# Reordering the stage between the projection and the attention of a hybrid decoder layer

## The reference

```
h = RMSNorm(x) * (1 + scale1(c)) + shift1(c)
p = h @ w_in
NSA group   (8 query heads, 2 kv heads): compressed-block, gathered top-k selected-block and
            sliding-window (512) branches, mixed by per-head sigmoid gates
mLSTM group (4 heads): matrix memory C, normaliser n, running-max stabiliser
pool group  (4 channel groups): trailing means over 2/4/8/16 positions, per-group linear map
x = x + gate1(c) * (concat(nsa, mlstm, pool) @ w_out)
h = RMSNorm(x) * (1 + scale2(c)) + shift2(c)
x = x + gate2(c) * ((silu(a) * b) @ w_down),  [a, b] = causal depthwise conv3(h @ w_up)
```

## Time and profile before

| | us |
|---|---|
| median of 3 runs (lowest, highest) | 848.26 (846.79, 848.85) |
| the profiled execution | 852.0 |
| its span in the trace | 850.1 |
| PE busy | 784.1 (92% of the span) |
| DVE busy | 508.4 (60%) |
| ACT busy | 329.0 (39%) |
| POOL busy | 307.6 (36%) |

### The profile page before, as it was taken

The page is one execution under the profiler, slowest core; times in us unless marked ns, Lnnn a source line. Parts: engine busy times, 40 slices in busy tenths (PEclk is TensorE's granted clock), DMA queues, the critical chain, the costliest instruction groups (busy, mean ns, idle before and its releaser), DMA issues.

```text
span 850.1 us, 18842 instructions
## 1 busy us (share of the span) xinstructions
PE 784.1 (92%) x7517; PEld 723.3 (85%) x7517; DVE 508.4 (60%) x1026; ACT 329.0 (39%) x601; POOL 307.6 (36%) x163
## 2 busy tenths in 40 slices
PE   2899989998989798998988999999999999999994
PEld 2798979988967565668988999999999999999993
DVE  3655888974494798763566566665212666665324
ACT  3332322322341356653235445443113455444221
POOL 0042656553000144461432344344444344343440
PEclk9899999998797699998999999999999999999997
DMA  9964867885569744305720333333323333322212
GB/s 354 332 214 136 252 221 254 288 263 163 201 217 385 141 120 122 102 2 174 292 98 28 122 105 120 114 105 105 94 81 112 123 101 112 100 78 97 89 56 100
DMA packets 73142, 131.23 MB, mean 154 GB/s; under 512 B 12685, under 2 KB 47389, under 8 KB 72801
## 3 DMA queue, kind: packets, MB, share of 16 engines
q1 hardware_dynamic: 66928, 114.32, 41.8%
q10 hardware_dynamic: 6096, 15.73, 5.2%
q0 software_dynamic: 32, 0.00, 0.0%
HBM read 124.56 MB, written 9.12 MB: 157 GB/s over the span
## 4 chain that ended last, share of the span: by engine, by line
PE 71%; DVE 12%; issue 6%; DMA 4%; POOL 3%; ACT 2%; SPq 2%; ACTq 0%; DVEq 0%; POOLq 0%
PE ps L668 53%; PE ps L1016 2%; PE ps L1001 2%; DMA arena<-cache_keys 2%; PE ps L1038 2%; POOL arena L612 2%; PE ps L1054 2%; PE ps L919 1%; DMA arena<-weights 1%; POOL wR L631 1%; PE ps L686 1%; DMA raw<-weights 1%; DVE arena L2079 1%; DVE arena L1504 1%; SPq L475 1%
## 5 line engine op out<-in xcount | busy, mean ns | idle before, releaser
L668 PE MATMUL ps<-hR,wR 128*128 128x260 f32 x3456 | 432.9, 287 | 11.5 <-POOL wR L631 3.6
L668 PEld LDWEIGHTS ps<-hR,wR 128*128 128x128 f32 x3456 | 426.2, 192 | 15.7 <-issue 10.7
L631 POOL TENSOR_TENSOR wR<-raw,wR 128x1024 fp32r<-128x1024 f32 x92 | 223.4, 2429 | 308.5 <-ACT wR L1136 308.5
L1136 ACT ACTIVATE wR<-raw 128x1024 fp32r<-128x1024 f32 x94 | 99.4, 1058 | 213.5 <-PE ps L668 210.0
L668 PE MATMUL ps<-fR,wR 128*128 128x260 f32 x1056 | 128.1, 283 | 2.2 <-DVE fR L2050 2.0
L668 PEld LDWEIGHTS ps<-fR,wR 128*128 128x128 f32 x1056 | 127.0, 188 | 3.1 <-DVE fR L2050 2.4
L2074 DVE COPY arena<-arena 128x2 f32<-128x2 f32 x44 | 47.6, 1082 | 93.6 <-ACT arena L1427 93.6
L624 POOL TENSOR_SCALAR arena<-arena,fac 128x128 f32<-128x128 f32 (+3 forms) x32 | 40.3, 1263 | 138.7 <-DVE fac L1973 138.7
L612 POOL TENSOR_TENSOR arena<-arena,par 128x512 f32<-128x512 f32 x32 | 43.6, 1369 | 72.7 <-DMA arena<-cache_keys 65.7
L2035 DVE TENSOR_TENSOR t<-ps,mod 128x8 f32<-128x8 f32 x24 | 4.0, 167 | 108.6 <-PE ps L668 108.6
L1360 ACT ACTIVATE arena<-ps,nmx 128x128 f32<-128x128 f32 (+3 forms) x64 | 33.2, 526 | 20.0 <-DVE nmx L1964 20.0
(11 more groups left out here) (369 smaller groups left out, 829.3 us busy)
## 6 DMA issues: line engine op xcount, KB each, us to landing
raw<-weights SPq DMA_DIRECT2D x95, 512.0 KB, 3.7
arena<-cache_keys SPq DMA_DIRECT2D x128, 192.0 KB, 3.5
arena<-weights SPq DMA_DIRECT2D x27, 512.0 KB, 9.5
arena<-cache_values SPq DMA_DIRECT2D x128, 64.0 KB, 2.0
raw<-weights ACTq DMA_DIRECT2D x12, 512.0 KB, 8.0
arena<-weights ACTq DMA_DIRECT2D x9, 512.0 KB, 7.5
x<-xT SPq DMA_DIRECT2D x16, 260.0 KB, 4.2
out_y<-x SPq DMA_DIRECT2D x8, 260.0 KB, 2.2
```

Source lines behind the costliest of these rows:

```text
L631: nc.gpsimd.tensor_tensor(w_slot(i)[:, 1, :, :], raw[:, g % RAW, :, :], w_slot(i)[:, 0, :, :].bitcast(F32), ALU.subtract).then_inc(lo_read ...
L668: last = mm(ps[:, a + half, 0:TH], w_slot(i)[:, wp, k, :], src[:, hp, j, half * TH:(half + 1) * TH], start=(j == 0 and q == 0), stop=(j == ...
L1136: A(w_slot(i)[:, 0, :, :], raw[:, g % RAW, :, :], ACT.Identity).then_inc(hi_ready, 1)
```

## The change

It leaves the arithmetic and moves instructions between the projection and the attention:

- PE: the block sums (L825) come ahead of triple 0; triples 1 to 7 stand earlier among the pieces, the gate columns behind the sample rows; the sample rows take 4 matmuls of 192 columns in place of 4 of 128 and 4 of 64; the pool group's map moves ahead of triple 7 and to other PSUM banks; the three last turns stand together, and the heads' transposes come last of all.
- DVE: the samples' block maxima and their ranking move forward, the compressed weights and the weighting of the samples' rows ahead of the last two heads; `side_mix` is gone, and the multiplication into `mix` is the last piece before L1900.
- SP: the gate rows leave before the window keys; the window keys go as six samples after the 15th half of the pages and two after the 16th (before: four and four after the 16th); SP issues the weight tiles of triples 2 to 7; the values of samples 0 and 1 come behind those; the window values of samples 0 and 1 now wait for `mmix_ready` and come before three weight tiles of the output projection and the small outputs.
- ACT: issues no weights, and its pieces follow PE's new order.

```diff
-            sp.wait_ge(comp_done, 2 * NB)
-            sp.wait_ge(slc_scored, 2 * NB)
-            for b in range(0, NB, 4):
-                sp.dma_start(kwin[:, b:b + 4, :], winK[:, b:b + 4, :]).then_inc(win_landed, 16)
+            sp.wait_ge(rows_ready, 1)
+            sp.dma_start(spread, mro[0:4, :]).then_inc(side_landed, 16)
+            for half, first, last in ((2 * NB - 1, 0, 6), (2 * NB, 6, 8)):
+                sp.wait_ge(comp_done, half)
+                sp.wait_ge(slc_scored, half)
+                sp.dma_start(kwin[:, first:last, :], winK[:, first:last, :]).then_inc(win_landed, 16)
...
+            load_rows(2)
+            load_rows(3)
+            for g in range(N_A + RAW + EXTRA, len(PART1)):
+                load_slot(g)
+
...
             sp.wait_ge(wsc_done, 2)
             load_values(0)
+            sp.dma_start(o_fm, pT[:, T_KC:T_MK, 0:S]).then_inc(early_out, 16)
+            sp.dma_start(o_vn, vn[:, :, :]).then_inc(early_out, 16)
             load_values(1)
             sp.dma_start(cst[:, :], mC).then_inc(rec_landed, 16)
...
+            sp.wait_ge(slot_done, len(PART1))
+            sp.wait_ge(mmix_ready, 1)
+            load_window(0)
+            load_window(1)
+            for g in range(len(PART1), len(PART1) + RAW):
+                load_slot(g)
...
+            def pooled_mix():
+
+                pe.wait_ge(pool_ready, 1)
+                pe.wait_ge(w_done, 4)
+                pe.wait_ge(wsc_evac, 3)
+                for t in range(2):
+                    mm(ps[:, 4 + t, :], par_("pw", t * P, (t + 1) * P), md[:, t, :], start=True, stop=True)
+                    last = mm(ps[:, 7, t * NB:(t + 1) * NB], par_("pw", t * P, (t + 1) * P), mds[:, t, :], start=True, stop=True)
+                last.then_inc(pool_mm, 1)
...
+            triple(4)
+            triple_turn(2)
+            window_rows()
+            triple(5)
             triple_turn(3)
-            triple(4)
             inside(2)
+            triple(6)
             triple_turn(4)
             inside(3)
-            triple(5)
+            pooled_mix()
+            triple(7)
             across(2)
             across(3)
             triple_turn(5)
...
             triple_turn(7)
+            head_turns()
...
-                for n in range(N_A + 3 * g, N_A + 3 * g + 3):
-                    if n in BEFORE:
-                        load_weights(BEFORE.index(n))
```

More of the change, by code:

```diff
@@ L810, in _ @@
             last.then_inc(blocks_done, 1)
[L811 to L819, removed]
             def block_sums():
@@ L833, in sample_rows @@
                     sel = every[:, 24 - 8 * hh:24 - 8 * hh + P]
-                    two = sn[0:NB, 0:512].rearrange("p (t h d) -> p t h d", t=2, h=4)[:, :, hh, :]
-                    mm(ps[:, 6, 0:P].rearrange("p (t d) -> p t d", t=2), sel, two, start=(hh == 0), stop=(hh == 3))
+                    three = sn[0:NB, 0:768].rearrange("p (t h d) -> p t h d", t=3, h=4)[:, :, hh, :]
+                    mm(ps[:, 6, 0:192].rearrange("p (t d) -> p t d", t=3), sel, three, start=(hh == 0), stop=(hh == 3))
                 for hh in range(4):
                     sel = every[:, 24 - 8 * hh:24 - 8 * hh + P]
[L838 to L841, removed]
+                    last = mm(ps[:, 6, 192:194], sel, sn[0:NB, 6 * P + hh:6 * P + hh + 33:32], start=(hh == 0), stop=(hh == 3))
                 last.then_inc(snew_done, 1)
+                pe.wait_ge(g_exp, 1)
+                for h in range(NH):
+                    last = mm(ps[0:64, 3, 400:403], pick[:, 7 - h:71 - h], sn[0:NB, 6 * P + 64 + 3 * h:6 * P + 67 + 3 * h],
+                              start=(h == 0), stop=(h == NH - 1))
+                last.then_inc(gates_done, 1)
             def compressed_scores():
@@ L930, in triple_turn, with head_turns @@
                 last.then_inc(ada_turned, 1)
+            def pooled_mix():
[6 more added lines that the diff above has]
+                last.then_inc(pool_mm, 1)
+            def head_turns():
+                pe.wait_ge(num_evac, 4)
+                for t in range(2):
+                    for i in range(ST):
+                        last = nc.tensor.transpose(ps[:, t, i * P:(i + 1) * P], hN[:, i, t * P:(t + 1) * P], ident)
+                last.then_inc(hT_done, 1)
+            block_sums()
             triple(0)
             compressed_scores()
-            gate_columns()
+            triple(1)
+            sample_rows()
             chunk_scores(0)
-            sample_rows()
-            block_sums()
             chunk_scores(1)
             triple_turn(0)
+            triple(2)
+            inside(0)
+            chunk_scores(2)
             window_scores(0)
-            triple(1)
-            inside(0)
+            inside(1)
+            triple_turn(1)
+            triple(3)
+            chunk_scores(3)
             window_scores(1)
[L944 to L951, removed]
             across(0)
             across(1)
+            triple(4)
+            triple_turn(2)
+            window_rows()
+            triple(5)
             triple_turn(3)
-            triple(4)
             inside(2)
+            triple(6)
             triple_turn(4)
             inside(3)
-            triple(5)
+            pooled_mix()
+            triple(7)
             across(2)
@@ L998, in scores @@
                 else:
-                    pe.wait_ge(side_mix, 1)
+                    pe.wait_ge(mmix_ready, 1)
                 for g in range(2):
@@ L1261, in _ @@
                 step(ev)
+            act.wait_ge(sx_in, 1)
+            A(scm[:, 0:NCB], scm[:, 0:NCB], ACT.Exp, bias=ssx[:, 1:2], scale=SCALE, accum_out=ssx[:, 2:3]).then_inc(sx_out, 1)
             act.wait_ge(kn_T, 1)
@@ L1666, in _, with samples_block_max @@
                     gate_maxima()
+            def samples_block_max():
+                for moved in sst_moved:
+                    dve.wait_ge(moved, 64 * NB // 2)
+                V.tensor_reduce(bmax[:, 0:32], sall[:, 0:NPG * P].rearrange("p (n k) -> p n k", k=64), AX, ALU.max)
             dve.wait_ge(blocks_done, NB)
@@ L1880, in _ @@
-            V.tensor_tensor(pc[:, :, 0:NCP], pc[:, :, 0:NCP], mx[:, 3, :].unsqueeze(2).broadcast_to([P, 32, NCP]), ALU.mult)\
-                .then_inc(pc_ready, 1)
-            dve.wait_ge(hT_done, 1)
-            windows_moved(dve)
-            V.tensor_tensor(mix[:, 4:6, 0:S], ps[:, 4:6, :], pT[:, T_MO:T_MO + 2, 0:S], ALU.mult).then_inc(mmix_ready, 1)
-            dve.wait_ge(pool_mm, 1)
-            for t in range(2):
-                V.tensor_scalar(mix[:, 6 + t, 0:S], ps[:, t, :], par_("pool_s", t, t + 1), None, ALU.mult)
-                last = V.tensor_scalar(mix[:, 6 + t, S:T], ps[:, 6, t * NB:(t + 1) * NB], par_("pool_s", t, t + 1), None, ALU.mult)
@@ L1892, in _ @@
[L1892 to L1898 removed]
+            samples_weights(1).then_inc(sp_ready, 1)
```

154 lines of the change are left out of this document (75 added, 79 removed).

## The result

The changed kernel took 858.45 us in the median of 7 runs (855.74 to 862.81), the kernel before 846.99 (844.87 to 852.42, 7 runs) beside it. The ratio is 1.0118, with an interval of 1.0096 to 1.0141: 1.2% slower, where 842.7 and 0.6% faster were forecast. Both kernels scatter by 7 to 8 us over these runs (by 10 to 16 on the later occasions), and their times go broadly with the mean clock that TensorE was granted in the run.

The account below looks back on a forecast made before the run. PE, partly at half clock, was taken to bound the stage and SP's queue what follows. Of 13.1 us gained 4.1 stay: -4.1 - 2.5 + 1.0 = -5.6 us, from the median 848.26 to 842.7; range 835.5 to 850.0.

Parts of the forecast that it names:

- DVE's idle time before the gate rows: Sign in the stage: gate rows leave before the window keys, so this idle time falls from 6.26 to about 1 us.
- PE's waits for weights: Sign in the stage: waits of 1.4 and 1.2 us vanish, as weights leave once their buffer is free.
- E: End of triple 5, where SP's later queue starts: forecast 250 us, S + 37.2 (S: the stage's first transposes).
- From E to the end of the stage: Remaining PE and DVE pieces behind triple 5: 17.6 us, ending the stage at 267.6.
- SP is the bound behind the stage: Claim that SP's issues come late next, so PE stands 9 us at sample 2.
- full-clock work before E: PE's work in the stage up to triple 5: 48.3 us less 14.9 behind it, giving 246.2 without waits.
- the clock's cost before E: Time lost to half clock before triple 5 ends: something over half of a 6.8 us stretch; bounds 0 and 13.5.
- my slower rival: Two full slow stretches make E 259.7, sample 2 starts at 320.7, total 852.4 us; chance 0.12.
- The queue from E on: SP's issues behind triple 5 until sample 2's window values land: E + 61.0, at 311.0 us.
- The small credit behind sample 2: DVE catches up while PE stands, 2.5 us gained, less 1.0 for the clock falling in the pause.
- A stage about 13.1 us shorter: Stage end forecast at 267.6 instead of 280.74; only 4.1 us of this was expected to remain at sample 2.
- SP does not bind: Rival behind the stage: issues faster or outputs nearly free, up to 13.1 us gained, 835 us; chance 0.10.

Follow-up runs that it names:

- e_issue: Kernel before with the changed kernel's SP queue, weights issued by SP, old order of PE, DVE and ACT: 860.23 us, ratio 1.0164 (4 runs).
- e_compute: Changed kernel's order of PE, DVE and ACT, with SP's queue of the kernel before and weights issued by ScalarE: median 850.95 us, ratio 0.9973.
- e_values: Changed kernel with ScalarE issuing the weights again, so values of samples 0 and 1 need not wait for triple 5: 850.33 us, ratio 1.0009.
- e_queue: e_window, plus sample outputs and window values 0 and 1 moved ahead of sample 1's pages, out_C behind sample 4: 847.11 us, ratio 0.9981.
- e_dense: Changed kernel with window scores of heads 0 moved right before triple 2, heads 1 right behind triple 3: 849.77 us, ratio 1.0024.
- e_both: Changed kernel with the SP queue of e_queue and the compute order of e_dense: 836.41 us, ratio 0.9885 to the kernel before (4 runs).
- e_after: The changed kernel itself, unaltered, measured again on the same chip as e_both_again: 860.67 us, ratio 1.0098 to the kernel before (10 runs).
- e_window: Changed kernel with SP issuing each sample's window values right behind its own values, from sample 2 on: 848.01 us, ratio 0.9995.
- e_both_again: The same kernel as e_both, with more runs: 837.69 us, ratio 0.9851 to the kernel before (6 runs).

## Why the prediction was wrong

**What held.** The 6.26 us of DVE's idle time before the gate rows went, and so did PE's waits for weights. With them went the slow stretch that began at S + 40.6 before, as I had assumed: where SP issues the weights, no profile has a stretch that begins between S + 16 and S + 50, not even that of e_issue with the old order, while e_compute and e_values, with weights by ScalarE and waits for them, have one of 10.2 us from S + 43. From E to the end of the stage 17.6 us were forecast, 18.0 measured. SP is the bound behind the stage: e_queue and e_values take the wait at sample 2 away. The full-clock work before E was forecast at 33.4 us; 46.9 less half of 30.6 is 31.6, 1.8 less; which piece I reckoned too dear no run singles out.

**The step that failed: the clock's cost before E.** I took 3.8 us (E = 250 for 246.2) and bounded it by 0 and 13.5. It was 15.3, half of 30.6 us, outside the bounds. My upper bound was the two slow stretches of the kernel before, on the silent assumption that the clock would come back between them as it had. But what stood where it had come back was just what the change moved: before, window scores and a triple adjoined there; in the new order the dense pieces each stand alone between thin ones. e_dense, which lets them touch again, has the stretch at 10.2 us, and E at S + 36.9. That this is near my S + 37.2 is partly luck: the clock cost it 5.1 us and not 3.8, and the work was less by about as much. The 11.5 us of clock that I had not put in, less those 1.8, are the first 9.7 us of the miss. It acted through the mechanism of my slower rival (a late E is added to the queue), whose E of 259.7 is S + 46.9 and was met to the tenth, though by one long stretch and not by two. That rival's 852.4 still lay 6 us under the measured median, by the two terms below (5.2 together) and by the differences between single executions. I gave that case 0.12, because I tied the second slow stretch to the waits for weights, and those did go.

**The queue from E on: 64.3 us instead of 61.0.** The two issues of `out_C` took 5.95 us instead of 4.42, and SP waited 3.6 us for outputs to land, `out_pool` last by the profile, before it could load the next page numbers and pages; I had not put that in. The two outputs behind the values of sample 0 took 3.5 us with their gaps, where I had 2.3. Against these 6.3 us stand shorter issues elsewhere (the 32 pages 19.90 for 20.8, the first 16 9.04 for 10.5, four small outputs 2.3 for 3.3) and a landing of 3.1 for 3.8; gaps of some tenths make up the rest. 9.7 late at E and 3.3 in the queue make 13.0, which takes sample 2 from the forecast S + 98.2 to S + 111.2.

**The small credit behind sample 2.** I took 1.5 us off (2.5 of DVE's arrears less 1.0 of clock). From sample 2 to the output projection it was 73.8 us before and 74.1 after: no credit, 0.4 lost. In e_queue and e_both, where PE does not stand, it was 72.8. The pause is paid for twice, as the clock falls in it and the stretch behind runs at half speed though PE is busy throughout:
```profile
321.95:330.00 8.05, 8.05 (x68) 4.85 (x70) 1.76 (x5) 0.83 (x2) 0.08 (x1) 0.50 0.41 116
```
From the forecast -5.6 us, then, +13.0 and +1.9 lead to +9.3, and 9.4 were measured at the start of the output projection.

**What the forecast had right about the gain.** A stage about 13.1 us shorter was nearly there to be had. In e_both, a kernel with other places and another queue than the one I forecast, it is 11.9 (67.9 less 56.0), and by the start of the output projection, with SP out of the way, the lead is 13.3 (176.0 less 162.7). My rival "SP does not bind" said 835; e_both, whose queue no longer binds, took 836.4 and 837.7. The Trainium skill (DMA: Bandwidth & Descriptors, Issuing engines are not separate DMA queues) calls the time to initiate a transfer usually small beside the transfer itself. Here issues filled some 52 of the 64.3 us behind E, and the 11.57 us that PE stood for the queue speak against it.

**What stays open.** Why the clock falls 13 to 16 us behind S in all the profiles with the new order, with PE busy without a break in nearly all of that time, and what makes the first stretch short or long with one and the same order, is not settled. The adjoining dense pieces are one way to shorten it (three profiles, all 10.2 us). They are not the only one: e_compute and e_values have the changed kernel's order of PE and were profiled with 6.8 and 10.2 us, and in the changed kernel the clock came back behind triple 4, which stands alone. A rival is untested: who issues the weights, and when. With that order and the weights issued by ScalarE 6 of 20 runs had a mean clock of 0.956 or more, with SP issuing them 2 of 37 (after, e_after, e_window, e_queue). What the runs show besides is the rate: in 17 runs of the changed kernel a mean clock of 0.947 or less 16 times; with the dense pieces adjoining and the queue mended 0.953 or more in all 10. The mean clock is one over the whole run, though, and the pause at sample 2 lowers it as well. How much each single output that e_queue moves is worth was not tried.

## What to carry to other kernels

Where a change puts a queue's issues behind a point of the computation, add up the issues from there to the first landing that somebody waits for, and treat that point as part of the critical path: here each microsecond of delay at triple 5 came out at sample 2, 64.3, 64.6 and (e_after) 64.1 us later. When pieces of TensorE are moved, look at the stretch table for the place at which the clock came back up, and ask whether the move takes that place apart; profile more than one run, as the length of a slow stretch can differ between runs of kernels with the same order. And test the two halves of a change alone: here the order alone was even in the half of its runs compared, the issues alone 1.6% slower (0.8 to 2.5, four runs), and the better parts of both 1.5% faster than the kernel before.

## What the runs showed of the hardware

The granted clock stayed at 0.50 for 30.6 us in which PE was busy without a gap, and moving pieces of some 1 to 2 us each shortened this to 10.2 us (e_dense, e_both, e_both_again). The Trainium skill (TensorE: Matmul & The Clock Gate, Why this matters for your kernels) asks for no long idle gaps between bursts of matmuls; these stretches had none, and the clock was down all the same. In the pause at sample 2, with PE idle, the clock fell too, 102.2 us behind S, and stayed down for 17.1 us, of which 8.05 were work (the row above), while e_queue and e_both, without the pause, have no slow stretch near it. One and the same kernel can take two ways: e_compute's ten runs split into two groups with medians 12 us apart and mean clocks of 0.952 to 0.964 and 0.941 to 0.946. The issue of one 64 KB page by SP took 0.57 us (9.04 for 16), 0.66 (21.02 for 32) and, in e_both behind the window values, 0.81 (13.01 for 16), so the length of a queue reckoned from one such row can be off by more than 20%. Two outputs of the matrix memory took 5.95 us to issue where they stood (DMA share there 1.12), and 1.23 in e_both behind sample 4 (share 0.65):
```profile
316.61 1.23 SPq L561 DMA_DIRECT2D out_C<-arena  x2
```
